# A decoder layer's state-space recurrence taken in chunks of four tokens, with attention spread over the gate tiles

## What is computed

```python
abar = exp(lambda * dt)                       # complex, one for each of 64 states of 64 groups
bbar = (abar - 1) / lambda * b
state[t] = abar * state[t-1] + bbar @ u[t]    # per group: 16 features in, 64 complex states
y[t] = Re(c @ state[t]) + d_skip * u[t]       # 16 features out
ssm_out = glu(gelu(y) @ w_glu)

q = rope(rms_norm(c_q) @ w_uq);  k, v = rms_norm(c_kv) @ w_ukv      # 16 heads
mla_out = causal_softmax(q @ k.T * scale) @ v
mix = (sigmoid(g_ssm) * ssm_out + sigmoid(g_mla) * mla_out) @ w_out
```

## Time and profile before

| | |
|---|---|
| time, median of 3 runs | 1525.12 us (1524.76 to 1529.2) |
| the profiled execution, its time | 1521.96 us |
| its span, first to last instruction | 1520.2 us |
| mean granted TensorE clock | 0.978 |
| PE, DVE, ACT, POOL busy | 1397.9, 991.2, 666.8, 94.7 us |
| DMA | 250.55 MB, mean 165 GB/s |

### The profile page before, as it was taken

How to read it: one execution, slowest core, us unless ns; L and a number is a source line. 1 busy time by engine, 2 the same in 40 slices (tenths; PEclk the granted TensorE clock), 3 DMA queues, 4 the chain that set the end, 5 groups by cost and what they waited for, 6 DMA issues and landing times.

```text
span 1520.2 us, 24054 instructions
## 1 busy us (share of the span) xinstructions
PE 1397.9 (92%) x8544; PEld 1228.4 (81%) x8544; DVE 991.2 (65%) x1394; ACT 666.8 (44%) x887; POOL 94.7 (6%) x41
## 2 busy tenths in 40 slices
PE   8997887887887969999888999999999999999996
PEld 7996776776776869988777888888888888888885
DVE  6666686796687776665786666666666664545455
ACT  5444354444443544443434444444444443333332
POOL 0000100100101100000280000000000000000002
PEclk9999999999999989999999999999999999999998
DMA  8542333332333337755435555555555565566562
GB/s 287 178 160 97 100 123 110 110 120 94 117 110 110 111 113 233 235 197 177 164 111 178 183 191 193 188 186 192 189 185 192 193 242 187 181 194 190 167 207 97
DMA packets 70683, 250.55 MB, mean 165 GB/s; under 512 B 7936, under 2 KB 8192, under 8 KB 70528
## 3 DMA queue, kind: packets, MB, share of 16 engines
q1 hardware_dynamic: 70656, 250.19, 50.2%
HBM read 248.06 MB, written 2.10 MB: 165 GB/s over the span
## 4 chain that ended last, share of the span: by engine, by line
PE 67%; DVE 19%; issue 6%; ACT 4%; DMA 3%; DVEq 0%; ACTq 0%; SPq 0%
PE ps L748 20%; PE ps L751 10%; PE ps L759 7%; PE ps L761 7%; PE ps L760 7%; PE ps L737 4%; PE ps L738 4%; PE ps L739 4%; DVE wlo L364 4%; DMA raw<-slabs 3%; DVE scan L1282 1%; ACT L516 1%; DVE scan L1281 1%; DVE prod L1273 1%; DVE prod L1265 1%
## 5 line engine op out<-in xcount | busy, mean ns | idle before, releaser
L426 ACT ACTIVATE whi<-raw 128x1024 fp32r<-128x1024 f32 x454 | 479.3, 1057 | 576.8 <-PE ps L761 208.5
L364 DVE TENSOR_TENSOR wlo<-raw,whi 128x1024 fp32r<-128x1024 f32 x430 | 537.1, 1256 | 293.9 <-ACT whi L426 293.5
L748 PE MATMUL ps<-hT,whi 128*128 128x512 f32 x1408 | 493.4, 393 | 10.5 <-DVE tmp L1555 9.8
L751 PE MATMUL ps<-hT,wlo 128*128 128x256 f32 x1408 | 398.9, 283 | 0.0
L748 PEld LDWEIGHTS ps<-hT,whi 128*128 128x128 f32 x1408 | 266.7, 189 | 68.1 <-DVE wlo L364 10.0
L751 PEld LDWEIGHTS ps<-hT,wlo 128*128 128x128 f32 x1408 | 268.2, 191 | 0.0
L737 PE MATMUL ps<-xT,whi 128*128 128x256 f32 x784 | 225.8, 288 | 31.6 <-DVE wlo L364 31.6
L738 PE MATMUL ps<-xT,whi 128*128 128x256 f32 x784 | 220.3, 281 | 0.0
L739 PE MATMUL ps<-xT,wlo 128*128 128x256 f32 x784 | 220.2, 281 | 0.0
L737 PEld LDWEIGHTS ps<-xT,whi 128*128 128x128 f32 x784 | 148.8, 190 | 46.5 <-DVE wlo L364 40.1
L738 PEld LDWEIGHTS ps<-xT,whi 128*128 128x128 f32 x784 | 148.9, 190 | 0.0
(11 more groups left out here) (205 smaller groups left out, 1616.9 us busy)
## 6 DMA issues: line engine op xcount, KB each, us to landing
raw<-slabs SPq DMA_DIRECT2D x454, 512.0 KB, 3.4
xrow<-x SPq DMA_DIRECT2D x4, 512.0 KB, 6.7
rows<-x SPq DMA_DIRECT2D x4, 512.0 KB, 5.5
gb<-ln_rows SPq DMA_DIRECT2D x4, 512.0 KB, 7.1
gb<-ln_rows SPq DMA_DIRECT2D x1, 2048.0 KB, 7.7
out<-rows SPq DMA_DIRECT2D x3, 256.0 KB, 2.5
out<-rows SPq DMA_DIRECT2D x2, 384.0 KB, 2.5
bpar<-ssm_b SPq DMA_DIRECT2D x1, 512.0 KB, 4.5
```

The lines of the kernel that those rows point to most:

```text
L364: unit.tensor_tensor(wlo[:, s, :], raw[:, s, :], whi[:, s, :].bitcast(F32), ALU.subtract).then_inc(done, 1 + empty_after)
L426: nc.scalar.activation(whi[:, s, :], raw[:, s, :], ACT.Copy).then_inc(hi_ready, 1 + empty)
L748: mm(ps[:, bank, :], hi, src[:, kt].rearrange("p a t -> p (a t)"), start=(first and n == 0), stop=False)
L751: ins = mm(ps[:, bank, TOK:512], lo, src[:, kt, 0, :], start=False, stop=done)
```

## The change

The recurrence now advances four tokens a step (`STEP = 4`, `NC = 64` steps), and a turn does its eight pairs at once (`PT = 8`). With j in 0..3 the token in a chunk:

- The chunk's four inputs are stacked on the partitions: `u4` holds, for each pair, 4 x 32 features by 64 chunks. ACT's `u_copy` writes u to `ustage` with the tokens sorted by j, and 16 DMAs of SP (`spread_u`) bring it into `u4`. They stand behind the load of slab 4 in the first head turn. The outputs take the way back by `gather_y`, 16 DMAs for six tiles behind slab 14 and 16 for two tiles behind slab 22 of the last turn. `d4` (D in the same layout) takes another 16 small DMAs early in the front.
- The weights are made in each turn. DVE forms A^e B in `wpad` (`b_mult`, `b_sums`) and C A^j in `ca` (`c_mult`, `c_sums`), ACT puts the bases in (`base`), POOL clears `wpad` at each turn; PE transposes `wpad` (`weight_turns`, 16 transposes), ACT copies them out (`weights_out`). `kernels` (16 matmuls) makes the direct part from input to output within a chunk, and ACT's `kernel_out` (10 small copies) places it in `kmat`. `s5_powers` makes the powers of A once, in the front.
- `b_product` is one set of 16 matmuls of 64 columns, `y_product` 24 of 64 columns; `turn_back`, `combine`, `turn_forward` run once a turn over 512 columns, `recur` is 16 scans of 64, `phases` and `trig` run once over 512 columns.
- The end of a turn has no `trig` and no gelu. Gelu runs after the loop on `yb`.
- PE's attention steps go by slabs instead of by gate tiles (`gate_half`): `turn_probs` and `score` after every third slab, `values` one slab later, `y_product` after the ninth.

```diff
+STEP = 4
+NC = TOK // STEP
+PT = PAIRS // HG
@@ SP
+            for b in range(STEP):
+                for q in range(4):
+                    sy.dma_start(d4[32 * b:32 * b + 32, q, :], cols[32 * q:32 * q + 32, P_D:P_D + UT]).then_inc(in_d, 16)
             load(7, 3, lo_dve, 4)
...
+            def spread_u():
+
+                sy.wait_ge(u_zero, 2)
+                for e in range(2):
+                    sy.wait_ge(tile_free[e], FREE0[e])
+                for b in range(STEP):
+                    j = (b + 1) % STEP
+                    for q in range(4):
+                        sy.dma_start(u4[32 * b:32 * b + 32, q:PAIRS:4, shift(b):shift(b) + NC],
+                                     ustage[32 * q:32 * q + 32, :, j, :]).then_inc(in_u, 16)
...
+            head_loads(0, {U_AT: spread_u})
+            with sy.Fori(1, HG - 1) as i:
+                head_loads(i)
+            head_loads(HG - 1, {Y_AT[0]: lambda: gather_y(0, UT - 2), Y_AT[1]: lambda: gather_y(UT - 2, UT)})
@@ ACT
-            trig(0, 0)
-            trig(0, 1)
...
                 latent(0, qT, 0)
                 latent(0, qT, 1)
                 hp(4)
...
+                base()
                 latent(0, qT, 2)
                 latent(0, qT, 3)
+                weights_out(0)
+                weights_out(1)
                 latent(2, kT, 0)
+                latent(2, kT, 1)
                 hp(6)
-                latent(2, kT, 1)
                 latent(2, kT, 2)
+                latent(2, kT, 3)
                 hp(7)
-                latent(2, kT, 3)
...
+                weights_out(2)
+                weights_out(3)
+                trig(i, 0)
+                trig(i, 1)
+                hp(8)
+                hp(9)
+                values_out()
+                hp(10)
+                kernel_out()
                 hp(11)
...
-                trig(i * 2 + 2, 0)
-                trig(i * 2 + 2, 1)
@@ PE
-            pe.wait_ge(b_padded, 6)
-            for c in range(2):
-                for q in range(2):
-                    for n in range(4):
-                        ins = nc.tensor.transpose(ps[:, BT_BANKS[2 * c + q], n * P:(n + 1) * P],
-                                                  bpad[:, c, (4 * q + n) * P:(4 * q + n + 1) * P], ident)
...
+                def b_product():
+
+                    pe.wait_ge(wb_ready, i * 4 + 4)
+                    pe.wait_ge(in_u, 16 * 16)
+                    for n in range(PT):
+                        for c in range(2):
+                            ins = mm(ps[:, BU + c, n * NC:(n + 1) * NC], wb[:, c, n, :],
+                                     u4[:, bass.ds(i * PT + n, 1), 0:NC].rearrange("p a k -> p (a k)"), start=True, stop=True)
...
+                kernels()
+                b_product()
                 score(0)
-                b_product(1)
-                gate_tile(0)
-                turn_probs(0)
...
+                for n in range(16):
+                    gate_half(n)
+                    if n % 3 == 2 and n < 12:
+                        turn_probs(n // 3)
+                        if n < 11:
+                            score(n // 3 + 1)
+                    if n % 3 == 0 and 0 < n < 13:
+                        values(n // 3 - 1)
+                    if n == 8:
+                        y_product()
@@ DVE
                 head_low(i, 2)
-                turn_back(0, 0)
-                turn_back(0, 1)
+                b_mult()
+                b_sums()
                 head_low(i, 3)
-                combine(0)
-                recur(0, 0)
-                recur(0, 1)
+                c_mult()
+                c_sums()
                 head_low(i, 4)
-                turn_forward(0, 0)
-                turn_forward(0, 1)
+                phases()
                 head_low(i, 6)
                 rotate()
                 head_low(i, 7)
+                rotate_sums()
                 head_low(i, 8)
...
+                head_low(i, 20)
+                y_out()
                 normalise(3)
                 head_out(2)
```

More of the change, by code:

```diff
@@ L560, in _, with values_out @@
+                def values_out():
+                    for t in range(2):
+                        if t == 0:
+                            ac.wait_ge(half_done, i * 6 + 6)
+                        else:
+                            ac.wait_ge(slab_used, i * HEAD_PER + HEAD0 + 8)
+                        nc.scalar.activation(vT[:, t, :], ps[:, t, :], ACT.Copy).then_inc(tile_free[t], 1)
                 latent(0, qT, 0)
@@ new lines, in _, with gelu, y_high @@
+            with ac.Fori(0, HG - 1) as i:
+                head_turn(i)
+            head_turn(HG - 1)
+            def gelu(m0, m1):
+                ac.wait_ge(in_y, 16 * 16 * (1 if m0 == 0 else 2))
+                nc.scalar.activation(yb[:, m0:m1], yb[:, m0:m1], ACT.Gelu_apprx_tanh).then_inc(y_act, 1)
+            def y_high(m):
+                ac.wait_ge(y_act, 1 if m < UT - 2 else 2)
+                ac.wait_ge(y_psum, HG)
+                nc.scalar.activation(yT[:, m, 0, :].rearrange("p (k j) -> p j k", j=STEP), yb[:, m], ACT.Copy).then_inc(y_hi, 1)
@@ L628, in glu_high @@
+            gelu(0, UT - 2)
+            for m in range(UT - 2):
+                y_high(m)
+            gelu(UT - 2, UT)
+            for m in range(UT - 2, UT):
+                y_high(m)
             def glu_high(i, k):
@@ new lines, in kernels @@
+                def kernels():
+                    pe.wait_ge(c_base, i * 2 + 2)
+                    pe.wait_ge(c_powers, i * 4 + 4)
+                    pe.wait_ge(y_ready, i * 2 + 1)
+                    for n in range(PT):
+                        g = n // 4
+                        for c in range(2):
+                            ins = mm(ps[32 * g:32 * g + 32, YP, (n % 4) * P:(n % 4 + 1) * P], wpad[:, c, n, P - 32:P],
+                                     ca[:, c, n, :], start=(c == 0), stop=(c == 1))
+                    ins.then_inc(k_psum, 1)
@@ L1157, in _ @@
                 set_up()
-            for v in range(12, 20):
+            for v in range(14, 20):
                 front_low(v)
@@ new lines, in y_out @@
+                def y_out():
+                    ve.wait_ge(y_psum, i + 1)
+                    parts = ((slice(0, P - 32), 1), (slice(P - 32, P), 0))
+                    for r, off in parts:
+                        u_ = u4[r, bass.ds(i * PT, PT), off:off + NC].rearrange("p (m q) k -> p m q k", q=4)
+                        d_ = d4[r, :, bass.ds(i * 2, 2)].rearrange("p q (m o) -> p m q o", o=1).to_broadcast([r.stop - r.start, 2, 4, NC])
+                        st(V.tensor_tensor(u_, u_, d_, ALU.mult))
+                    st.wait()
+                    for r, off in parts:
+                        u_ = u4[r, bass.ds(i * PT, PT), off:off + NC]
+                        V.tensor_tensor(u_, u_, of_pairs(ps[r, YP, :]), ALU.add).then_inc(y_ready, 1)
```

537 lines of the change are left out of this document (269 added, 268 removed).

## The result

The changed kernel takes 1460.06 us (median of 4, 1458.54 to 1462.19) against 1525.93 us (1524.76 to 1529.2) for the kernel before: ratio 0.9566, 95% interval 0.9546 to 0.9586. The forecast was 1466, with a range of 1440 to 1495. The profiled execution has a span of 1458.6 us, where before had 1520.2.

The account below looks back on a forecast made before the run. PE bounds the kernel, waiting mostly for DVE, late because of the recurrence. Savings of 55.4 (loop), 1.7 (front) and 1.4 (behind) make 58.5 us: 1521.96 becomes 1463.5, plus 3.2 for the median, rounded to 1466; range 1440 to 1495.

Parts of the forecast that it names:

- four turns without the transfers: Head loop: four turns of 95.3 us each, 381.2 in all, before anything is added for spread_u and gather_y.
- `spread_u` and `gather_y`: SP's small transfers in the first and last head turns: 3 us added for all three sets together.
- the loop: The four head turns: from 439.5 us to 384, a saving of 55.4.
- the front: Before the head loop: the 16 transposes of B go, 1.7 us less; nothing taken for d4's issues.
- PE's gap behind the loop: Between the head loop and PE's next work: 6.41 us becomes 5.0, so 1.4 less.
- The turn: One head turn: PE busy for 92.2 us plus 3.1 idle, 95.3 in all.
- the clock's term: PE's slow slabs after gaps in a turn: 0.8 us saved for the value slab, 1.5 for the latent slab.
- The small waits of 1.5: PE's idle time in a turn: 1.5 us for small waits that couldn't be placed, beside 1.6 for rotate.
- 64 columns: PE's 40 small recurrence matmuls a turn: 9.0 us at the 128-column price, the upper value taken; 4.5 if proportional to columns.
- The scans: DVE's 16 scans of 64 columns a turn: 0.2 us each, 3.2 in all.
- Small packets: Rival on the 256-byte SBUF transfers: stalls could eat all 58.5 us; slower 4%, a loss of 30 us or more 8%.
- In-order waits: Rival: DVE and ACT wait in order for PE in each turn, 27 us more, 1493; 14%.

Follow-up runs that it names:

- b_short: Kernel before, with DVE's recurrence operations on 32 of every 256 columns: 1482.58 us, ratio 0.973.
- a_extra40: Kernel after, with 40 more DVE operations of 512 columns a turn, eight at each of five places: 1535.79 us, ratio 1.0063.
- b_notrig: Kernel before, with trig at a turn's end replaced by three copies of one column: 1514.33 us, ratio 0.9934.
- a_d4: Kernel after, with the 16 d4 transfers one behind each of 16 front loads from slab 8 on: 1456.28 us, ratio 0.9546.
- a_split: Kernel after, with SP's 16 + 16 + 16 transfers for u4 and yb cut into pieces of four behind slab loads: 1447.37 us, ratio 0.9485.
- a_one: Kernel after, with each of three sets of 16 transfers made one transfer of the same bytes in 256-byte runs: 1447.48 us, ratio 0.9487.

## Why the prediction was right, and where it was off

The mechanism held. DVE was late because of the recurrence, and without that PE's waits for it vanish; `b_short` shows it from the other side. `a_extra40` gives the whole gain back by loading DVE again, though by another wait: 37.4 us over the loop are for `mla` and 3.8 for `wlo`. It shows that DVE's time at those places counts, not that the old waits return. The predicted gain was 58.5 us of the profiled execution, measured 61.6 there and 65.9 between the medians. That closeness is in part luck, for terms were off in both directions:

| term | predicted | measured |
|---|---|---|
| four turns without the transfers | 381.2 | 361.2 (4 x 90.3) |
| `spread_u` and `gather_y` | +3 | +13.8 (4.9 + 8.9) |
| the loop | -55.4 | -64.4 |
| the front | -1.7 | +1.3 |
| PE's gap behind the loop | -1.4 | -0.7 |
| behind it | 0 | +2.1 |

The two small terms at the ends can't be read from one pair of executions. The loop starts at 116.75 to 118.4 us in five profiled executions with the front of before, and at 117.3 to 119.7 in seven with the front of after; behind the loop they take 957.6 to 959.1 and 958.6 to 959.9.

**The turn.** PE's work was set at 92.2 us and is 88.7; idle at 3.1 and is 1.6. The recurrence itself was priced well: 1.6 for the transposes, 3.2 for `kernels`, 3.6 for `b_product` and 5.3 for `y_product`, 13.7 against 14.3. What I had too small is what PE gets back when it doesn't stop. PE stopped 16 times for 0.15 us or more in the second turn of before and stops once now; at 0.16 us for each of 15 that is 2.4, where I took ten. The value slabs run at full clock even behind the 1.58 us gap (two slabs, 24 matmuls of 512 columns, in 5.86, where the 12 of one took 4.60), so the clock's term is about 1.8 there and not 0.8. These give 0.6 + 0.8 + 1.0, 2.4 of the 3.5; the rest I can't place. The small waits of 1.5 that I couldn't name do not exist. DVE is busy for 61.1 us of a turn, where I had 58; two operations that ran beside POOL (last section) take 4.0 of it more than their neighbours, at no cost to PE.

**`trig`.** Its place at the turn's end is worth 10 us by `b_notrig`, 4.1 of them behind the loop, where the change itself gains only 0.7. The change doesn't clear ACT at the turn's start altogether, as the part on the change has it: a table load of 1.28 us still stands ahead of the first `latent` (`L596`, at 214.67 us in the second turn), and PE has no wait for `qT` there.

**64 columns.** The upper bound was right: `L962`, `L964` and `L965` start 0.22 us apart, as do matmuls of 128 columns:

```profile
277.34 0.39 PE L962 MATMUL ps<-u,kmat 128*128 x2
277.56 0.39 PE L964 MATMUL ps<-prod,ca 128*128 128x64 f32 x2
277.79 0.39 PE L965 MATMUL ps<-prod,ca 128*128 128x64 f32 x2
```

By the rule of the Trainium skill (TensorE: Matmul & The Clock Gate, Back-to-back issue gap) they would have been near 0.12, by the estimate in the prediction. I had left out that this section gives the rule for an isolated matmul and says that with few columns it counts too little where weights are loaded for each. The measurement agrees with that and decides: 0.22 us with new 128 x 128 f32 weights for every 64 columns.

**The scans.** Eight of 64 columns take 1.57 us together, 0.19 each, against 0.2 taken.

**The transfers.** This is the step that failed: "So it costs nothing by 3 us", and for the front "the slabs already in the ring give PE 8.6 us of work". The issues took 0.73 (`u4`) and 0.64 us (`yb`) each, not 0.5, so `spread_u` ended at 129.7 instead of 125, and ACT's copy of slab 6 began at 133.31, where I had the slab landed by 128. And the slack was measured to the wrong point. I asked when PE needs the slab, but ACT's order asks for it sooner: its copy of that slab stands ahead of evictions that PE needs for slabs it already has. In the front, 16 issues took 8.45 us, 0.53 each, little over the 7 to 8 forecast and under the 8.6 of work in the ring, and PE stopped all the same, through that path: 2.1 us of gap and some 1.7 of slower clock, 3.8 by `a_d4`. For the last turn the forecast had "the second ends close to the last slab" and a turn of 95; ACT's copy of that slab stands before `copy_pt`, which PE wanted at 474.9 us (481.31 less 6.40), 81 us into the turn. Each stop costs more than its gap: 2.65 us in the first turn stand for 4.9 (with 0.4 for `qT`), and `a_split` gives back 12.7 us for 9.1 us of waits.

**The rivals.** Small packets: wrong, shown by `a_one`. The rule of the Trainium skill on transfers within SBUF (DMA: Bandwidth & Descriptors, Why small descriptors are slow (HBM only)) agrees. Nor did the transfers run one after another: each of `spread_u` landed 2.2 us after its issue (median), and the next was issued 0.65 us after it. In-order waits: they exist, but on ACT behind late slabs, 13.8 us in place of the 27 of that case. On DVE they lie close: 14 us of additional work a turn bring 27 us back.

How the 66 us divide: relief of DVE alone brought 41 in the kernel before, the order of attention 9 in the kernel after, the trig at the turn's end 10 in the kernel before. The three were measured in different kernels, so that they come to 60 is no proof of a sum.

## What to carry to other kernels

When an engine with in-order work makes the bound engine wait, look at what stands between two of its deliveries, not only at its busy share: here DVE was idle for 29 us a turn, and 14 us more of work, set ahead of `head_out` and other steps, still cost 6.8 us. What the same work costs at other places was not run. A group of small DMAs costs its issues, and everything behind them on that queue is late by their sum; spread them over the loads, a few at a time, or make them one. To find the slack of a load, follow the engine that touches it first and what is queued behind it there, not the engine that uses it last.

## What the runs showed of the hardware

An f32 matmul on new 128 x 128 weights takes 0.22 to 0.23 us at 128, at 64 and at 32 columns. At 32 columns in `b_product` the granted clock fell in two turns of four, to 0.71 and 0.68 in the windows of 2.8 us behind, though PE did not stop there; at 64 it stayed at 1.00.

A DVE operation of 512 columns from and to SBUF took 2.86 us, and another 2.54, where its neighbours take 0.68; so in all four turns. Each ended 0.55 us after a low part of POOL that ran at the same time (252.61 to 255.72, with the first):

```profile
253.41 2.86 DVE L1401 TENSOR_TENSOR prod<-prod 128x512 f32<-128x512 f32 x1
256.20 0.68 DVE L1402 TENSOR_TENSOR prod<-prod 128x512 f32<-128x512 f32 x1
...
252.61 3.12 POOL L411 TENSOR_TENSOR wlo<-raw,whi 128x1024 fp32r<-128x1024 f32 x1 [11.52 <-ACT whi L479]
```

POOL's part took 3.12 to 3.17 us there and 2.34 to 2.40 elsewhere in the loop. It began there while a low part of DVE was running (252.28 to 253.50 in this case), and that one kept its usual 1.22 us. So in each pair the one that started later was longer. That the two share something is only argued; no run took it apart.
